# Layer 1's memory softmax tiles turned on VectorE instead of TensorE, in a two-layer decoder trunk

## The reference, cut to what matters

```python
def _memory_attention(q, mem_n, w_kv, q_g, k_g):
    ...
    scores = jnp.einsum("bshd,bmhd->bhsm", q, k).astype(jnp.float32) * (MEM_HEAD_DIM ** -0.5)
    p = jax.nn.softmax(scores, axis=-1).astype(v.dtype)
    o = jnp.einsum("bhsm,bmhd->bshd", p, v)
    return o.reshape(b, s, MEM_WIDTH)

def _sb_mix(h, mem_n, w_in, q_g, k_g, w_out, mem_w_kv, mq_g, mk_g):
    ...
    o = _stick_breaking(q, k, v.reshape(shp)).reshape(b, s, SB_WIDTH)
    o_mem = _memory_attention(q_mem, mem_n, mem_w_kv, mq_g, mk_g)
    return jnp.concatenate([o, o_mem], axis=-1) @ w_out
```

## Time and profile before

| | |
|---|---|
| median of 3 runs | 798.12 us (798.07 to 798.46) |
| the profiled execution | 799.2 us |
| its span, first to last instruction | 797.3 us |
| TensorE busy | 792.1 us, 99% |
| VectorE busy | 613.0 us, 77% |
| ScalarE busy | 435.7 us, 55% |
| GpSimd busy | 72.8 us, 9% |
| granted TensorE clock | 1.000 over the span |

### The profile page before, as it was taken

How to read it: one execution, slowest core, us unless ns; L and a number is a source line. 1 busy time by engine, 2 the same in 40 slices (tenths; PEclk the granted TensorE clock), 3 DMA queues, 4 the chain that set the end, 5 groups by cost and what they waited for, 6 DMA issues and landing times.

```text
span 797.3 us, 9715 instructions
## 1 busy us (share of the span) xinstructions
PE 792.1 (99%) x3742; PEld 659.2 (83%) x3742; DVE 613.0 (77%) x923; ACT 435.7 (55%) x518; POOL 72.8 (9%) x94
## 2 busy tenths in 40 slices
PE   9999999999999999999999999999999999999998
PEld 6988888888888888888888888888888888888886
DVE  5688999987758788888748878758666778888862
ACT  5677774566537454444327576766653735445430
POOL 4010032520000000000000000123330000000000
PEclk9999999999999999999999999999999999999999
DMA  7854456533446656655646545442445566565551
GB/s 246 291 163 158 160 197 217 192 131 112 157 157 209 202 180 199 200 181 199 208 162 202 170 157 161 157 159 105 159 147 164 168 209 185 187 209 191 181 209 53
DMA packets 85309, 141.38 MB, mean 177 GB/s; under 512 B 3422, under 2 KB 50688, under 8 KB 85264
## 3 DMA queue, kind: packets, MB, share of 16 engines
q1 hardware_dynamic: 84272, 139.60, 53.5%
q10 hardware_dynamic: 608, 1.06, 0.4%
q0 software_dynamic: 384, 0.11, 0.1%
HBM read 139.68 MB, written 1.07 MB: 177 GB/s over the span
## 4 chain that ended last, share of the span: by engine, by line
PE 89%; DVE 7%; ACT 2%; issue 2%; POOL 0%; DVEq 0%; POOLq 0%
PE acc L1331 27%; PE acc L1333 27%; PE acc L1332 27%; PE bank L1328 3%; DVE lo L999 2%; PE acc L1538 1%; ACT hi L686 1%; PE bank L1519 1%; PE bank L1497 1%; DVE hg L1123 1%; ACT sq L686 1%; PE bank L1509 1%; PE bank L1474 0%; PE bank L1491 0%; ACT p L686 0%
## 5 line engine op out<-in xcount | busy, mean ns | idle before, releaser
L999 DVE TENSOR_TENSOR lo<-raw,hi 128x2048 fp32r<-128x2048 f32 (+2 forms) x130 | 292.6, 2256 | 74.7 <-ACT hi L686 73.5
L686 ACT ACTIVATE hi<-raw 128x2048 fp32r<-128x2048 f32 (+2 forms) x130 | 242.6, 1873 | 87.0 <-DMA raw<-in_ffn_w_gate_up 44.5
L1331 PE MATMUL acc<-lo,aT_hi 128*128 128x512 f32 (+1 forms) x664 | 259.2, 390 | 0.4 <-DVE lo L999 0.4
L1333 PE MATMUL acc<-hi,aT_lo 128*128 128x512 f32 (+1 forms) x664 | 255.5, 385 | 0.0
L1332 PE MATMUL acc<-hi,aT_hi 128*128 128x512 f32 (+1 forms) x664 | 255.1, 384 | 0.0
L1331 PEld LDWEIGHTS acc<-lo,aT_hi 128*128 128x128 f32 x664 | 124.7, 188 | 25.3 <-DVE lo L999 0.9
L1333 PEld LDWEIGHTS acc<-hi,aT_lo 128*128 128x128 f32 x664 | 124.6, 188 | 25.0
L1332 PEld LDWEIGHTS acc<-hi,aT_hi 128*128 128x128 f32 x664 | 124.8, 188 | 24.4 <-issue 0.2
L1210 DVE STREAM_TRANSPOSE uT<-un 32x256 f32<-32x256 f32 (+1 forms) x192 | 79.4, 413 | 3.1
L1331 PE MATMUL acc<-lo,uT_hi 128*128 128x512 f32 x176 | 68.6, 390 | 0.0
L1333 PE MATMUL acc<-hi,uT_lo 128*128 128x512 f32 x176 | 68.5, 389 | 0.0
(11 more groups left out here) (210 smaller groups left out, 859.7 us busy)
## 6 DMA issues: line engine op xcount, KB each, us to landing
raw<-in_ffn_w_gate_up SPq DMA_DIRECT2D x88, 512.0 KB, 4.8
raw<-in_ffn_w_down SPq DMA_DIRECT2D x22, 1024.0 KB, 4.9
raw<-in_sb_w_in SPq DMA_DIRECT2D x20, 1024.0 KB, 5.1
raw<-in_ssd_w_in SPq DMA_DIRECT2D x14, 1024.0 KB, 5.2
raw<-in_mem_w_kv SPq DMA_DIRECT2D x8, 1024.0 KB, 5.0
raw<-in_ssd_w_out SPq DMA_DIRECT2D x8, 1024.0 KB, 4.9
raw<-in_sb_w_out SPq DMA_DIRECT2D x8, 1024.0 KB, 4.9
seg<-cs_rows SPq DMA_DIRECT2D x6, 384.0 KB, 4.8
```

What stands on the lines that cost most here:

```text
L686: return nc.scalar.activation(out_, in_, func, **k)
L999: v.tensor_tensor(lo[w % RING][:, c], raw[w % RING][:, c], hi[w % RING][:, c].bitcast(F), ALU.subtract).then_inc(lo_ready, 1)
L1331: mm(ps, stat_hi, mov_lo, start=first, stop=False)
L1333: return mm(ps, stat_lo, mov_hi, start=False, stop=last)
```

## The change

- The steps `pT` of layer 1 are replaced by `pq`, which only VectorE does: for half of the token columns of a head pair's four 128x128 tiles, eight instructions, each turning eight squares of 32x32 on 32 partitions (256 numbers a partition), straight from `kmT[0]` or `vm[0]` into `pmT[1]`. TensorE's sixteen transposes and ScalarE's four copies are gone, and the PSUM banks that they took as well.
- `pq` stands behind units 80, 82, 85 and 88. The first of a pair waits for the last scores, or for the first pair's value products, since it writes over `hg`.
- `mo` stands behind units 84 and 90 and waits for both steps of its pair.
- `OUT1_ROWS` takes rows 14 and 15 at its fourth place (unit 92) instead of its second.

```diff
--- before.py
+++ after.py
@@ -61,7 +61,7 @@
 FFN_PAIRS = (FFN_BLOCKS + 1) // 2
 
 OUT0_ROWS = [12, 0, 14, 2, 4, 6, 8, 10]
-OUT1_ROWS = [12, 14, 0, 2, 4, 6, 8, 10]
+OUT1_ROWS = [12, 0, 2, 14, 4, 6, 8, 10]
 DOWN_ROWS = list(range(0, HT, 2))
 
 U_IN0 = 0
@@ -154,8 +154,8 @@
             at(u, ("sc", l, hp, t))
             at(u + 1, ("pn", l, hp, t))
         for hp in range(2):
-            at(u_p[2 * hp], ("pT", l, 2 * hp))
-            at(u_p[2 * hp + 1], ("pT", l, 2 * hp + 1))
+            for i in range(2):
+                at(u_p[2 * hp + i], ("pq", hp, i) if l else ("pT", l, 2 * hp + i))
             at(u_o[hp], ("mo", l, hp))
 
         for steps in PLAN.values():
@@ -190,7 +190,7 @@
     for n in ("qm1", "k0", "k1", "k2", "q0", "q1", "q2"):
         at(block_end(n) + (4 if n == "q2" else 2), ("hT", n, 0), ("hT", n, 1))
     k = block_end("qm1") + 4
-    memory_attention(1, (k, k + 2, k + 2, k + 4), (k + 5, k + 5, k + 8, k + 8), (k + 6, k + 12))
+    memory_attention(1, (k, k + 2, k + 2, k + 4), (k + 6, k + 8, k + 11, k + 14), (k + 10, k + 16))
     for n in HEAD_NORMS[1:-1]:
         at(block_end(n) + 1, ("hn", n))
     at(block_end("q2") + 2, ("hr", "q2"))
@@ -202,7 +202,7 @@
 
 
 
-NO_BANK = ("gate", "silu", "seg", "segm", "pn", "dt", "memsq", "memnorm", "sps", "zd", "hn", "hr", "hm", "tq", "ts")
+NO_BANK = ("pq", "gate", "silu", "seg", "segm", "pn", "dt", "memsq", "memnorm", "sps", "zd", "hn", "hr", "hm", "tq", "ts")
 
 EARLY, MIDDLE = ("seg", "pn", "zd", "sps", "hn"), ("segm",)
 USES = {s: i for i, s in enumerate(s for u in sorted(PLAN) for s in PLAN[u] if s[0] not in NO_BANK)}
@@ -891,8 +891,6 @@
                     wait_full(act, step)
                     if h >= 2:
                         wait_full(act, ("mo", l, 0))
-                    elif l == 1:
-                        wait_full(act, ("sc", 1, 1, 1))
                     read(step, f(pmT[l][:, h % 2].rearrange("p m t -> p (m t)"), T(step)[:]))
                 elif kind == "mo":
                     _, l, hp = step
@@ -1188,6 +1186,18 @@
                     pv = pm[l][2 * hp + t]
                     v.tensor_tensor(pv, pv, each(rsum, MEM), ALU.mult).then_inc(S("p_normed"), 1)
                     dve.wait_ge(S("p_normed"), i + 1)
+                elif kind == "pq":
+                    _, hp, half = step
+                    if half == 0:
+                        wait_full(dve, ("mo", 1, 0) if hp else ("sc", 1, 1, 1))
+                    pair = (kmT, vm)[hp][0][:].rearrange("p a (b n) -> p (a b n)", n=P)
+                    rows = pair.rearrange("p (t k n) -> p t k n", t=TOK, n=P)
+                    cols_ = pmT[1].rearrange("p h m (t n) -> p t (h m) n", n=P)
+                    for b in (2 * half, 2 * half + 1):
+                        for a in range(4):
+                            last = v.transpose(cols_[32 * b:32 * b + 32, :, :, 32 * a:32 * a + 32],
+                                               rows[32 * a:32 * a + 32, :, :, 32 * b:32 * b + 32])
+                    last.then_inc(S("p_turned"), 1)
                 elif kind == "mo":
                     _, l, hp = step
                     dve.wait_ge(S("mo_hi"), 2 * l + hp + 1)
@@ -1484,7 +1494,10 @@
                     _, l, hp = step
                     wait_acc_read_all(BLOCK_ACC[f"vm{l}"])
                     for h in range(2):
-                        wait_read(pe, ("pT", l, 2 * hp + h))
+                        if l == 0:
+                            wait_read(pe, ("pT", l, 2 * hp + h))
+                    if l == 1:
+                        pe.wait_ge(S("p_turned"), 2 * hp + 2)
                     for h in range(2):
                         c0 = (2 * hp + h) * P
                         for m in range(2):
```

## The result

The changed kernel takes **799.95 us** (median of 11 runs, 799.43 to 800.46), the kernel before 798.10 us beside it (11 runs, 797.53 to 799.77): a ratio of 1.0021, with its 95% interval 1.0014 to 1.0029. So it is slower by 1.85 us, small but resolved. 800.2 was forecast, with 797.6 to 801.8 as the range, and slower as the likeliest direction. The profiled execution is the one of 799.95 us, with a span of 798.0 us (before: 799.2 and 797.3).

The account below looks back on a forecast made before the run. TensorE's own issued work was taken as the bound, VectorE as only just ahead. The terms -1.76 + 0.35 + 2.3 + 1.2 = +2.1 us gave 800.2 us, with an 8-in-10 range of 797.6 to 801.8.

Parts of the forecast that it names:

- TensorE loses 1.76 us: Units 79 and 82: two groups of eight transposes leave TensorE's queue, 0.88 us each, so -1.76 us.
- The moves cost nothing: Value products moved behind units 84 and 90, output rows reordered: no cost by themselves, only TensorE early in between.
- The transposes take 0.45 us each: VectorE's 32 transposes at 0.45 us each, 3.6 us per step of eight; bounds 0.435 and 0.477 us.
- The value products take 1.6 us: A head pair's value products on TensorE: 1.54 us to the next, slow product, taken as 1.6 us; moved, not removed.
- First gap, +2.65: Behind units 82 and 83: TensorE waits for VectorE, +0.35 for `lo` of unit 83 and +2.3 for `sp_lo`.
- Second gap, +1.2: Behind units 86 and 87: third step delays VectorE; TensorE waits for `C`, partly earlier at banks `zd` reads, +1.2 us.
- Fourth step, no cost: Ends about 564.7 us, `sp_lo` at 565.7; `C` of heads 6 and 7 has 1.0 us of cover, so free.
- VectorE has room enough: Rival: VectorE's idle time in both gaps absorbs the transposes, only -1.76 counts: 796.4 us; 9%.
- Only one gap: Rival: only one gap opens; first alone gives 799.0 us, second alone 797.6 us; 17%.
- The change doesn't do what it says: Rival: some leftover wait keeps the value products in their old places; with something worse than all this, 3%.
- The transposes hold up GpSimd: Rival: transposes delay GpSimd's mask over `spb`, then `sp_hi`, `sp_lo` and `C`: 1.5 us more, 801.7 us; 5%.

Follow-up runs that it names:

- the change again: The changed kernel, unaltered, timed a second time beside the kernel before: 799.87 us, ratio 1.0023.
- 8 eights, later: Changed kernel with whole steps of eight transposes behind units 83, 85, 88 and 90, value products behind 86 and 92: 798.76 us, ratio 1.0004.
- the first experiment: Kernel before with layer 1's softmax tiles turned by no engine, its memory attention left out of the result: 797.22 us, ratio 0.9972.
- the third: Kernel before with the change's product places and row order; TensorE still turns, behind units 79 and 86 where banks are free: 798.23 us, ratio 1.0000.
- fourth: Changed kernel with every second transpose left out, four instead of eight a step, half of each tile unturned: 797.56 us, ratio 0.9982.
- sixth: Changed kernel with first pair's products behind unit 86, second pair's transposes behind 88 and 90, products behind 92, rows 14 and 15 sixth: 798.57 us.
- seventh: Changed kernel with transposes in eight steps of four, behind units 82 to 85 and 88 to 91, products behind 86 and 92: 797.10 us, ratio 0.9986.
- second experiment: Kernel before with the change's product places and row order; TensorE still turns, behind units 80, 82, 85 and 88: 806.17 us, ratio 1.0082.
- fifth: Changed kernel with each step's eight transposes done twice, the second eight behind a wait for the first: 818.42 us, measured once.

## Why the forecast held, point by point

The times of the stretch (us against before, one profile each) and the medians. The medians' differences lie within 0.5 us of the stretch's:

| kernel | stretch | median and its partner before |
|---|---|---|
| the change | +1.75 | 799.95, 798.10 |
| the change again | +1.80 | 799.87, 797.93 |
| 1 no turning | -1.76 | 797.22, 799.13 |
| 2 moves, bank in use | +7.46 | 806.17, 799.13 |
| 3 moves, bank free | +0.03 | 798.23, 798.17 |
| 4 half turned | -1.09 | 797.56, 799.13 |
| 5 turned twice | +19.72 | 818.42, 799.13 |
| 6 first gap only | +0.78 | 798.57, 797.93 |
| 7 pieces of four | -1.18 | 797.10, 797.93 |
| 8 eights, later | +0.43 | 798.76, 798.17 |

**TensorE loses 1.76 us.** Right; the first experiment gives 1.76. (TensorE's busy time fell by 1.2, not by 1.8. But it is 790.9 in one profile of the changed kernel and 790.4 in that of the repeat, which is why the stretch is the better measure.)

**The moves cost nothing.** Right, by the third.

**The transposes take 0.45 us each.** Right: 3.56 to 3.60 us for eight in a row. The destination's extra level costs nothing that shows.

**The value products take 1.6 us.** Mis-sized: 1.72. Where a pair's products now stand, the offset grows by 1.72 and 1.74 us. The rows behind unit 84 say where 1.72 comes from, before without them and after with them:

```profile
527.70 0.38 PE L1520 MATMUL bank<-lsb,vn 128*128 128x128 f32 x2
527.84 0.48 PE L1331 MATMUL acc<-lo,aT_hi 128*128 128x512 f32 x1
528.16 0.40 PE L1332 MATMUL acc<-hi,aT_hi 128*128 128x512 f32 x1
```

```profile
525.67 0.38 PE L1533 MATMUL bank<-lsb,vn 128*128 128x128 f32 x2
525.89 1.89 PE L1504 MATMUL bank<-hg,vm 128*128 128x256 f32 x8
527.43 0.58 PE L1341 MATMUL acc<-lo,aT_hi 128*128 128x512 f32 x1
527.85 0.40 PE L1342 MATMUL acc<-hi,aT_hi 128*128 128x512 f32 x1
```

From the last row of `O` to the second product of the unit it is 0.46 us before and 2.18 after: 1.72 more. I had taken the 1.54 us to the next product and rounded up a little, without the later start of the products themselves. The third experiment shows the same size, a lead of 2.60 us = 1.72 + 0.88. The term cancels in the sum, since the products are moved and not removed, but it makes TensorE 0.12 us earlier in both gaps than I had it.

**First gap, +2.65.** Right in kind, 2.52 measured: TensorE would be 1.76 + 1.72 = 3.48 us ahead without waits and is 0.96 ahead with them. The smaller term, 0.35 for `lo` of unit 83, was put at the wrong unit. TensorE waits for `lo` of unit **81**, and not for that of 83. I had the row in hand: `lo` of units 81 and 82 are the two operations of 494.86 and 4.49 us in the earlier trace rows. The first ends at about 497.1, and a TensorE that is early by 2.6 us wants it at 499.24 - 2.6 = 496.6 (499.24 is the first product of unit 81 in the timeline of before). I followed only the end of the second. This costs 0.5 us, and it takes away the wait at unit 83, since TensorE then comes later. The larger term, 2.3 for `sp_lo`, measured 2.03. TensorE wanted `sp_lo` at 518.13 - 2.03 = 516.10, in before's times (+1.06) 517.16, where I had 517.15. That this agrees is luck: the lead was larger by 0.12 us and the first wait by 0.15. `sp_lo` ended at 519.09 in before's times instead of 519.35, and `C` starts 0.10 us behind it, as I had it. The two terms aren't independent, either. VectorE doesn't wait between the two steps, so the end of `sp_lo` alone sets when `C` starts; what TensorE loses at `lo` of unit 81 it would otherwise have lost at `C`.

**Second gap, +1.2.** Right in its mechanism, by the third, fourth and sixth experiments, and mis-sized: 0.97 us. The offset would go from 0.76 to 0.76 - 1.72 = -0.96, and +0.01 is measured; the sixth experiment gives 0.97 as well. The term that was mis-sized is my chain of VectorE's durations, which I laid end to end. From the start of `C` behind 85 to the end of `sp_lo` I had 15.71 us (535.54 to 551.25), and it takes 15.33 (534.34 to 549.67). About 0.1 us of that is my rounding. The rest is that an operation of VectorE can start a little before the end shown for the one before it: `oT_lo` from 544.17 with 0.74 ends at 544.91, and the sum behind it starts at 544.83. That is 0.08 us, and the chain has three such places. The waits fall where I said, at the bank that `zd` reads: 0.8 us of PEld behind unit 86, in two, and at `C` behind unit 87 only 0.1 to 0.2 are left.

**Fourth step, no cost.** Right: `C` behind 89 holds its offset, +0.01 as behind 87.

With the products at 1.72 the sum closes: -1.76 + 2.52 + 0.97 = 1.73, against 1.75 measured. The forecast of 2.1 was 0.35 us too high, 0.13 in the first gap and 0.23 in the second, and both mostly for VectorE's chain, which runs a little faster than its durations laid end to end.

**The rivals.** *VectorE has room enough* falls by the result, and the fourth and seventh experiments say how: it has, for steps of 1.8 us and not of 3.6. *Only one gap* falls by the sixth. *The change doesn't do what it says* falls by the rows at 525.89 and 572.95. *The transposes hold up GpSimd* falls by two rows of GpSimd in the changed kernel. The first answers to the earlier trace rows:

```profile
511.29 2.71 POOL L652 TENSOR_TENSOR spb<-spb,tlt 128x256 f32<-128x256 f32 x1 [0.32 <-DVE spb L1242]
...
539.03 0.74 POOL L652 TENSOR_TENSOR lsb<-lsb,tlt 128x256 f32<-128x256 f32 x1 [13.40 <-ACT lsb L686]
```

The first met `lo` of unit 84 (511.13 to 513.41) as before, and ended at 514.00, within the transposes of 513.44 to 517.04. It came 0.59 us after `lo` had ended, as it did in the earlier trace rows. The second, a mask of the same size on `lsb`, lies wholly within the third step of transposes (536.25 to 539.81) and took 0.74 us. So the transposes didn't hold them. The Trainium skill, page "SBUF — State Buffer", section "Who interferes with whom", has a VectorE instruction with at most one SBUF input, outside the two-port modes, leave GpSimd alone; the trace agrees with it here.

**A correction.** The text ahead of the prediction counts a head's tiles as four 128x128 tiles of two passes, and the prediction sets "0.88 us of TensorE against 3.6 us of VectorE for the same half pair". A head pair has eight 128x128 tiles in all. A group of eight TensorE transposes (0.88 us) turns the whole pair, one instruction a tile (the changed kernel has sixteen fewer, for two pairs), and VectorE needs two steps for the pair, 7.2 us. Per tile that is 0.11 us against 0.9, a ratio of 8 and not 4. The sum went by groups and steps as they are issued, so it doesn't change; but the price of the trade was stated at half of what it is.

## What to carry to other kernels

Work that is taken off the bounding engine makes that engine early at its next meeting with each of the others; reckon the slack of every result there, from the first one on, and give the work back to the helper in pieces no longer than the idle stretch it is to lie in. Here the same transposes cost 1.75 us in pieces of eight at the places of the change and 0.43 at later places, and gained 1.18 in pieces of four there. Where buffers go round in a fixed turn, a step that takes one inherits the wait for whoever reads it last, and a step that takes none can be moved freely. And a difference of 0.2% is best read between two rows that both traces share, with the medians as a check.

## What the runs showed of the hardware

The granted clock of TensorE fell to 0.50 (1.2 GHz) at single standstills of 3.73 us (second experiment) and of 3.91, 3.69 and 2.50 us (fifth), and behind a pair of 1.91 and 1.14 us that ended 2.2 us apart (fifth). It stayed at 1.00 behind the 1.79 us of the changed kernel, where TensorE was busy for 0.34 of 2 us:

```profile
516.00:518.00 2.00, 0.34 (x3) 0.15 (x1) 1.94 (x5) 0.68 (x1) 0.00 (x0) 1.00 0.89 222
518.00:520.00 2.00, 1.87 (x10) 1.69 (x11) 2.00 (x2) 0.60 (x2) 0.00 (x0) 1.00 0.78 302
```

So a wait can cost more than its length: the 3.73 us of the second experiment brought 2.7 us more behind them, by the accounting given there.

VectorE's `lo` takes 2.28 or 2.29 us, also where GpSimd's mask comes upon it; there the mask took 2.71 us instead of 0.74. Where the mask was running first, `lo` took 2.90. The two rows, of VectorE and of GpSimd in the changed kernel:

```profile
524.88 2.90 DVE L997 TENSOR_TENSOR lo<-raw,hi 128x2048 fp32r<-128x2048 f32 x1 [0.84 <-ACT hi L686]
```

```profile
524.21 1.43 POOL L652 TENSOR_TENSOR spb<-spb,tlt 128x256 f32<-128x256 f32 x2
```

The masks lie from 524.21 to 525.64, and `lo` starts inside them. Its extra 0.61 us is a little less than the 0.76 us from its start to the end of the masks. It isn't the only such row: the kernel before has four in layer 0 (2.61, 2.91, 2.65 and 2.78 us, from 116.48, 139.80, 156.74 and 191.03), each begun while an operation of GpSimd was under way. It cost nothing here.
